# Product-key router of a 2-layer mixer block: the remaining up tiles beside the router in joined form, leading weights on VectorE, every second low part on GpSimd

## The chip, the core and the metric

One core of a Trainium2 chip runs the whole program. The metric is device time in microseconds (us), the median of three runs. Engines are called by the profile's names: PE is TensorE (PEld its weight loads), DVE is VectorE, ACT is ScalarE, POOL is GpSimd, SP is the queue that issues the weight transfers from HBM.

## The reference

Two stacks of two layers are run one after the other on 256 tokens of width 1024. The first stack has a product-key expert layer (PEER) after each mixer, and the change touches those two alone. Cut to what matters:

```python
def peer_mixer(h, w_query, sub_keys, w_up, w_down):
    q = (xc @ w_query).reshape(c, 8, 2, 128)
    sc = einsum('chpd,hpnd->chpn', q, keys32)
    sv, si = top_k(sc, 16)
    cand = sv[:, :, 0, :, None] + sv[:, :, 1, None, :]
    best, pos = top_k(cand, 16)
    eidx = ...                       # one of 128 x 128 experts, 8 x 16 of them a token
    g = softmax(best)
    a = einsum('cd,chkd->chk', xc, w_up[eidx])
    act = gelu(a) * g
    return einsum('chk,chkd->cd', act, w_down[eidx])
```

## The kernel before

**Dense experts.** The kernel does not gather. It computes `a` for all 16384 experts and multiplies by a weight that is zero for those not chosen. An "up tile" t (0 to 127) is 128 experts: its 128x1024 weights are loaded as one unit of 512 KB by SP into `raw`, a ring of 4. The program computes in fp32 accuracy with split numbers: ACT copies `raw` into `wh` (the high part, `high(n)`, line 1525), DVE writes `wl = raw - wh` (the low part, `low(n)`, line 2000). `wh` and `wl` are rings of two. The tokens are split in the same way and lie side by side in `x_both`. PE makes wh x high tokens, wh x low tokens and wl x high tokens.

**Two forms of an up tile** (`up(t)`). The joined form multiplies each of the 8 slices of `wh` with high and low tokens in one matmul of 512 columns (line 1148), then the 8 slices of `wl` with the high tokens, 256 columns each (line 1152). The bank then holds two halves that must be added: ACT copies both to `halves` (`copy_halves`, line 1650), POOL adds them (line 837, or line 849 into `late_sum`), and ACT applies gelu. The separate form runs 16 + 8 matmuls of 256 columns (line 1160) that all add up in one half, and ACT applies gelu right out of the bank.

**The stage of the change.** Tiles 72 to 127 (`FIRST` is 72) run beside the router. Of these, `LATE_JOINED` holds the even ones from 72 to 124, so 27 of the 56 tiles are joined and 29 separate, turn by turn. The router turns the chosen keys and weights of 4 tokens (a "quad", 64 in all) into a 128x128 table of weights for each token: it is a product of two one-hot matrices, one of them multiplied by the weight in three bf16 parts. For a quad, `build(q)` on DVE makes the one-hots (line 2318) and puts on the second and third part (two instructions, line 2324); `weigh_first(q)` on ACT puts on the leading part (four instructions, line 1719); PE makes 12 matmuls (`router(q)`, line 1189); ACT moves weights of later tiles to `acts` (`hold`, line 1727); DVE multiplies what is there already (`weigh`, line 2334, reading a PSUM bank) and tile by tile the rest (`late_weigh`, line 2343). The one-hots are a ring of 4 quads (`RING`), the weighted ones of 3 (`FIRSTS`), the router's banks of 4 (`OUTS`). The router of 2 or 3 quads stands in PE's order after every second (odd) tile: `quads_after(k)`.

**Order.** Every engine runs its own instructions in the order of the code. In the loop over `k` (tile 72 + k) ACT runs: copy or gelu of the tile, `weigh_first` of the next quads, `high` of tile + 2, late gelu of a joined tile, `hold`. DVE runs: `build` of the quads of slot k + 1, `low` of tile + 1, then at every second k `weigh` of 2 or 3 quads, then `late_weigh` of the tile before. POOL only adds the halves. SP loads a unit again when `lo_ready` has counted the unit four before it. After the stage come the down tiles (line 1176), which need all weights to be in place.

Of the kernel before, what the change touches and what calls it, by code (L numbers as in the profile page):

```python
# [13 lines left out]
F32 = mybir.dt.float32  # L14
# [8 lines left out]
P = 128  # L23
# [68 lines left out]
RING, FIRSTS, OUTS = 4, 3, 4  # L92
FIRST, SLOTS = 72, 54
APART = (range(22, 30), range(52, 60))
LATE_JOINED = range(FIRST, N_KEYS - 2, 2)
SPANS = ((0, 22), (22, 30), (30, 52), (52, 60), (60, FIRST))
EXP_TILES, SUM_TILES, CHOICE_TILES = (26, 54), (31, 61), (35, 63)
WIDE, NARROW = 4, 4
# [159 lines left out]
def build(nc, d, out):  # L258
    ctx = ExitStack()
    with ctx:  # L260
# [5 lines left out]
        def sem(name):  # L266
            if name not in sems:
                sems[name] = ctx.enter_context(nc.semaphore(name))
            return sems[name]
# [55 lines left out]
        at = place_of["aux"]  # L325
        lanes = place("lanes", [P, N_KEYS], BF16, at)
        at += 2 * N_KEYS
        weight_high = place("weight_high", [P, SEQ], F32, at)
        at += 4 * SEQ
        key_pairs = place("key_pairs", [P, SEQ, 2, 2], BF16, at)  # L330
        at += 2 * 4 * SEQ
        rest_pairs = place("rest_pairs", [P, 2, SEQ, 2], BF16, at)
        at += 2 * 4 * SEQ
        onehot = place("onehot", [P, RING, QUAD, 2, N_KEYS], BF16, at)
        at += 2 * RING * QUAD * 2 * N_KEYS
        first = place("first", [P, FIRSTS, 3, QUAD, N_KEYS], BF16, at)
# [205 lines left out]
        top_ready, top_exp = sem("top_ready"), sem("top_exp")  # L542
        top_split = sem("choices_split")
        onehots, first_weighted = sem("onehots_ready"), sem("first_keys_weighted")
        rests_weighted = sem("first_keys_weighted_by_rests")
        products, weighted = sem("router_products"), sem("experts_weighted")
        held, late_weighted = sem("router_weights_held"), sem("late_experts_weighted")
        gelu_done = sem("gelu_done")
# [229 lines left out]
        def _(pool):  # L778
# [47 lines left out]
            for layer, done in enumerate(("wo", "conv")):  # L826
                row_scales(f"peer{layer}")

                pool.dma_start(view(P_KEYS, HP, N_KEYS), d["keysT"][layer])\
                    .then_inc(extra_loaded["keys"], 16)  # L830
                pool.wait_ge(x_low, XG[f"rescaled{layer}"] + 4)
                pool.dma_start(lanes[:], d["c_lanes"].partition_broadcast(P)).then_inc(extra_loaded["lanes"], 16)

                def sum_halves(t, i=0):

                    pool.wait_ge(up_copied, unit_wait(joined(layer, t) + 1, i))
                    pool.tensor_tensor(acts[:, bass.ds(i * 4 + t, 1), :].rearrange("p a b -> p (a b)"), halves[:, 0], halves[:, 1], ALU.add)\  # L837
                        .then_inc(up_summed, 1)

                for c0, c1 in SPANS:  # L840
                    if together(c0):
                        with pool.Fori(0, (c1 - c0) // 4) as i:
                            for t in range(c0, c0 + 4):
                                sum_halves(t, i)
                        for t in range(c1 - (c1 - c0) % 4, c1):
                            sum_halves(t)
                for t in LATE_JOINED:
                    pool.wait_ge(up_copied, joined(layer, t) + 1)
                    pool.tensor_tensor(late_sum[:], halves[:, 0], halves[:, 1], ALU.add).then_inc(up_summed, 1)
                dump(done)  # L850
                if layer == 1:

                    pool.wait_ge(weighted, QUADS * (layer + 1))
                    pool.dma_start(gain_bc, d["norm_final"].partition_broadcast(P)).then_inc(extra_loaded["gain"], 16)
                    pool.dma_start(inv_freq, d["c_inv_freq"].partition_broadcast(P)).then_inc(extra_loaded["masks"], 16)
                    pool.dma_start(causal, d["c_causal"]).then_inc(extra_loaded["masks"], 16)
                    pool.dma_start(cmp_mask, d["c_cmp_mask"]).then_inc(extra_loaded["masks"], 16)
                    pool.wait_ge(units_used, first_unit["down1"] + HALF)
                    for t in range(TT):
                        pool.dma_start(view(0, TT, D)[:, t, :], d["mem"][t * P:(t + 1) * P, :])\  # L860
                            .then_inc(extra_loaded["mem"], 16)
                    row_scales("mem")
                row_scales(("conv", "between")[layer])
                dump(("peer0", "peer1")[layer])
# [30 lines left out]
        def _(pe):  # L895
# [213 lines left out]
            def peer(layer):  # L1109
# [27 lines left out]
                def up(t, i=0):  # L1137

                    n, b = u0 + t, t % 2
                    w = [x[:, n % SPLIT, :].rearrange("p (k e) -> p k e", k=KT) for x in (wh, wl)]  # L1140
                    if t >= 2 and together(t - 2):
                        pe.wait_ge(up_copied, unit_wait(joined(layer, t - 1), i))
                    elif t >= 2:
                        pe.wait_ge(gelu_done, unit_wait(N_KEYS * layer + t - 1, i))
                    if together(t):
                        pe.wait_ge(hi_ready, unit_wait(n + 1, i))
                        for k in range(KT):
                            pe.matmul(banks[b].rearrange("p (a b) -> p a b", a=2), lhsT=w[0][:, k, :], rhs=x_both[:, :, k, :],  # L1148
                                      start=k == 0, stop=False, skip_group_check=True)
                        pe.wait_ge(lo_ready, unit_wait(n + 1, i))  # L1150
                        for k in range(KT):
                            last = pe.matmul(banks[b][:, 0:SEQ], lhsT=w[1][:, k, :], rhs=xh[:, k, :], start=False, stop=k == KT - 1,  # L1152
                                             skip_group_check=True)
                        last.then_inc(units_used, 1)
                        return
                    for part in range(2):
                        pe.wait_ge((hi_ready, lo_ready)[part], unit_wait(n + 1, i))
                        for k in range(KT):
                            for xp in range(2 - part):
                                last = pe.matmul(banks[b][:, 0:SEQ], lhsT=w[part][:, k, :], rhs=x_in[xp][:, k, :],  # L1160
                                                 start=(k == 0 and part == 0 and xp == 0), stop=(k == KT - 1 and part == 1))
                    last.then_inc(units_used, 1)
# [18 lines left out]
                def router(q):  # L1181

                    pe.wait_ge(first_weighted, q0 + q + 1)
                    pe.wait_ge(rests_weighted, q0 + q + 1)
                    if q >= OUTS:
                        pe.wait_ge(weighted, q0 + q - OUTS + 1)
                    for c in range(QUAD):
# [317 lines left out]
        def _(act):  # L1505
# [113 lines left out]
            def peer(layer):  # L1619
# [89 lines left out]
                        ins = act.activation(acts[:, t, n:SEQ], src[:, n:SEQ], ACT.Gelu)  # L1709
                    ins.then_inc(gelu_done, 1)  # L1710

                def weigh_first(q):

                    act.wait_ge(onehots, q0 + q + 1)
                    if q >= FIRSTS:
                        act.wait_ge(products, q0 + q - FIRSTS + 1)
                    for c in range(QUAD):
                        c0 = q * QUAD + c
                        ins = act.activation(first[:, q % FIRSTS, 0, c, :], onehot[:, q % RING, c, 0, :], ACT.Copy,  # L1719
                                             scale=weight_high[:, c0:c0 + 1])  # L1720
                    ins.then_inc(first_weighted, 1)

                def hold(q):

                    n = tiles_before(q)
# [11 lines left out]
                    src = acts[:, bass.ds(i * 4 + t, 1), :].rearrange("p a b -> p (a b)")  # L1737
                    act.activation(gated_parts(layer, t)[0], src, ACT.Copy).then_inc(g_high, 1)

                for q in quads_in(0):  # L1740
                    weigh_first(q)
                for k in range(N_KEYS - FIRST):
                    if FIRST + k in LATE_JOINED:
                        copy_halves(FIRST + k)
# [2 lines left out]
                    if FIRST + k == N_KEYS - 2:  # L1747
                        act.wait_ge(weighted, q0 + QUADS)
                        gated_high(0)
                    for q in quads_in(k + 1):  # L1750
                        weigh_first(q)
                    high(u0 + FIRST + k + SPLIT)
                    if FIRST + k in LATE_JOINED:
                        late_gelu(FIRST + k)
# [224 lines left out]
        def _(dve):  # L1979
# [139 lines left out]
            def peer(layer):  # L2119
# [118 lines left out]
                def weights_of(t):  # L2238

                    cols = slice(t * P, (t + 1) * P)  # L2240
                    dve.tensor_copy(weight_high[:, cols], rounded[:])
                    step(tt(rest_of, choice[:, 2], rounded[:], ALU.subtract))
                    step(dve.tensor_copy(rest_pairs[:, 0, cols], rest_of.unsqueeze(2).to_broadcast([P, P, 2])))
                    step(tt(rest_of, rest_of, rest_pairs[:, 0, cols, 0], ALU.subtract))
                    step(dve.tensor_copy(rest_pairs[:, 1, cols], rest_of.unsqueeze(2).to_broadcast([P, P, 2])))

                wait_read(dve, J.of(f"scores{layer}", 7))
                dve.wait_ge(extra_loaded["lanes"], 16 * (layer + 1))
# [60 lines left out]
                def build(q):  # L2309
# [9 lines left out]
                    dve.wait_ge(onehots, q0 + q + 1)  # L2319
                    if q >= FIRSTS:  # L2320
                        dve.wait_ge(products, q0 + q - FIRSTS + 1)
                    for p in range(2):
                        rest_w = rest_pairs[:, p, c0:c0 + QUAD].unsqueeze(2).to_broadcast([P, QUAD, w, 2])
                        last = tt(first[:, q % FIRSTS, 1 + p].rearrange("p c (n b) -> p c n b", b=2),  # L2324
                                  onehot[:, s, :, 0].rearrange("p c (n b) -> p c n b", b=2), rest_w, ALU.mult)
                    last.then_inc(rests_weighted, 1)

                def weigh(q):

# [25 lines left out]
                for k in range(N_KEYS - FIRST):  # L2355
                    for q in quads_in(k + 1):
                        build(q)
                    low(u0 + FIRST + k + 1)
                    if k:
                        for q in quads_after(k - 1):  # L2360
                            weigh(q)
# [586 lines left out]
```

## Time and profile before

| | |
|---|---|
| median of 3 runs | 2298.92 us (2298.03 to 2300.6) |
| profiled execution | 2300.05 us |
| its span | 2298.2 us |
| busy PE / PEld / DVE / ACT / POOL | 2281.4 / 1996.9 / 1677.7 / 1404.6 / 181.4 us |
| chain that ended last | PE 92%, DVE 5%, issue 1%, ACT 1% |

"Busy" is the time in which an engine had at least one instruction under way. Matmuls overlap, so a busy PE is not a PE at its peak: the distance between starts says what one costs. The same holds on a smaller scale for DVE, whose next instruction starts some 80 ns before the end of the last. The chain follows the last instruction back, at each step to what released it. The stage beside the router occupies 387.4 to 591.9 us in the first PEER layer and 1295.0 to 1499.5 us in the second.

### The profile page before, as it was taken

What the parts mean: (1) busy time and instruction counts of PE and PEld (TensorE: products, weight loads), DVE (VectorE), ACT (ScalarE), POOL (GpSimd) and SP (SyncE); (2) the same over time, 40 slices, a digit from 0 to 9 for tenths busy, and PEclk for the clock granted to TensorE, in tenths of its full rate; (3) what the DMA queues carried; (4) which work ended last, traced back from release to release, by engine and by line L of the source; (5) the groups of instructions that cost most, each with busy time, mean ns of one, the idle gap of its engine ahead of it and who ended that gap; (6) DMA issues with size and microseconds to landing.
All of it is one profiled execution on the core that took longest, in us unless ns stands there. A gap on an engine that the chain in (4) does not pass through costs nothing.

```text
span 2298.2 us, 42511 instructions
## 1 busy us (share of the span) xinstructions
PE 2281.4 (99%) x14253; PEld 1996.9 (87%) x14253; DVE 1677.7 (73%) x3045; ACT 1404.6 (61%) x2618; POOL 181.4 (8%) x257
## 2 busy tenths in 40 slices
PE   9999999999999999999999999999999999999998
PEld 8799999999888888999899999988888888788777
DVE  6767997999655555775999799966555668767565
ACT  5657666888544455446666788844555555665554
POOL 1002121111000000000211211100000010000000
PEclk9999999999999999999999999999999999999999
DMA  7455666444566666566566544466666654346454
GB/s 244 146 185 163 187 183 181 142 144 141 184 193 193 195 192 192 177 183 192 168 182 190 166 141 146 147 207 192 191 211 181 194 187 136 86 139 197 131 165 146
DMA packets 137470, 397.50 MB, mean 173 GB/s; under 512 B 12480, under 2 KB 13808, under 8 KB 136560
## 3 DMA queue, kind: packets, MB, share of 16 engines
q1 hardware_dynamic: 134448, 384.71, 54.9%
q0 software_dynamic: 2448, 10.56, 1.4%
q8 instruction: 86, 1.41, 0.2%
q14 instruction: 56, 0.46, 0.1%
q10 hardware_dynamic: 432, 0.36, 0.0%
HBM read 394.54 MB, written 1.05 MB: 172 GB/s over the span
## 4 chain that ended last, share of the span: by engine, by line
PE 92%; DVE 5%; issue 1%; ACT 1%; DVEq 0%; POOLq 0%; POOL 0%; ACTq 0%
PE bank L1176 29%; PE bank L1148 13%; PE bank L1004 13%; PE bank L1160 11%; PE bank L1010 7%; PE bank L1152 7%; PE bank L1189 4%; DVE wl L2000 2%; PE bank L1036 1%; PE bank L1252 1%; PE bank L1104 1%; PE bank L1128 1%; PE bank L1015 0%; DVE aux L2038 0%; PE bank L1080 0%
## 5 line engine op out<-in xcount | busy, mean ns | idle before, releaser
L2000 DVE TENSOR_TENSOR wl<-raw,wh 128x1024 fp32r<-128x1024 f32 x726 | 886.8, 1223 | 501.2 <-ACT wh L1525 488.3
L1525 ACT ACTIVATE wh<-raw 128x1024 fp32r<-128x1024 f32 x725 | 764.4, 1055 | 602.2 <-PE bank L1176 327.7
L1148 PE MATMUL bank<-x_both,wh 128*128 128x512 f32 x1328 | 337.4, 396 | 0.0
L1148 PEld LDWEIGHTS bank<-x_both,wh 128*128 128x128 f32 x1328 | 238.2, 189 | 42.7
L1176 PE MATMUL bank<-wh,gl 128*128 128x512 f32 x992 | 265.6, 389 | 0.0
L1176 PE MATMUL bank<-wh,gh 128*128 128x512 f32 x992 | 265.3, 389 | 0.0
L1176 PE MATMUL bank<-wl,gh 128*128 128x512 f32 x992 | 265.2, 389 | 0.0
L1176 PEld LDWEIGHTS bank<-wh,gl 128*128 128x128 f32 x992 | 185.9, 188 | 39.5 <-DVE gl L2349 1.0
L1176 PEld LDWEIGHTS bank<-wl,gh 128*128 128x128 f32 x992 | 186.2, 188 | 38.8
L1176 PEld LDWEIGHTS bank<-wh,gh 128*128 128x128 f32 x992 | 186.0, 188 | 38.4
L1004 PE MATMUL bank<-wh,x_both 128*128 128x512 f32 (+1 forms) x768 | 195.9, 397 | 0.2 <-DVE x_both L2046 0.2
L1152 PEld LDWEIGHTS bank<-x_both,wl 128*128 128x128 f32 x1328 | 180.8, 190 | 14.6 <-DVE wl L2000 1.7
L1650 ACT ACTIVATE halves<-bank 128x512 f32<-128x512 f32 x166 | 99.3, 598 | 150.4 <-PE bank L1152 150.1
L1160 PE MATMUL bank<-x_both,wh 128*128 128x256 f32 x1440 | 188.3, 284 | 0.1
L1152 PE MATMUL bank<-x_both,wl 128*128 128x256 f32 x1328 | 185.5, 282 | 0.1
L1160 PEld LDWEIGHTS bank<-x_both,wh 128*128 128x128 f32 x1440 | 179.0, 192 | 1.0 <-ACT arena L1643 0.9
L1004 PEld LDWEIGHTS bank<-wh,x_both 128*128 128x128 f32 x768 | 140.0, 189 | 33.4 <-issue 6.3
L1719 ACT ACTIVATE first<-onehot,weight_high 128x128 bf16<-128x128 bf16 x512 | 160.7, 394 | 1.7 <-PE bank L1189 1.5
L2324 DVE TENSOR_TENSOR first<-onehot,rest_pairs 128x512 bf16<-128x512 bf16 x256 | 100.4, 433 | 20.3 <-PE bank L1189 16.3
L837 POOL TENSOR_TENSOR arena<-halves 128x256 f32 (+1 forms) x112 | 85.5, 763 | 358.2 <-ACT halves L1650 358.2
L2349 DVE TENSOR_TENSOR gl<-arena,gh 128x256 fp32r<-128x256 f32 x252 | 105.3, 418 | 0.0
L1004 PE MATMUL bank<-wl,x_both 128*128 128x512 f32 (+1 forms) x384 | 103.0, 390 | 0.0
(334 smaller groups left out, 2876.8 us busy)
## 6 DMA issues: line engine op xcount, KB each, us to landing
raw<-in_w_upT SPq DMA_DIRECT2D x256, 512.0 KB, 3.6
raw<-in_w_down SPq DMA_DIRECT2D x256, 512.0 KB, 3.7
raw<-in_l_w_in SPq DMA_DIRECT2D x84, 512.0 KB, 3.7
raw<-in_peer_w_query SPq DMA_DIRECT2D x32, 512.0 KB, 3.8
raw<-in_l_w_out SPq DMA_DIRECT2D x28, 512.0 KB, 3.7
raw<-in_conv_w_in SPq DMA_DIRECT2D x24, 512.0 KB, 3.8
raw<-in_attn_w_qkv SPq DMA_DIRECT2D x23, 512.0 KB, 4.6
arena<-in_na_bias POOLq DMA_DIRECT2D x4, 1024.0 KB, 6.2
```

The costliest lines, as they stand in the source:

```text
L1004: last = pe.matmul(bank(js[b])[:, 0:cols], lhsT=x[:, kt, b * P:(b + 1) * P], rhs=w[part][:, kk, :], **flags)
L1010: last = pe.matmul(bank(js[b])[:, m * SEQ:(m + 1) * SEQ], lhsT=w[part][:, kk, c0:c0 + P], rhs=x[:, kt, :], **f)
L1148: pe.matmul(banks[b].rearrange("p (a b) -> p a b", a=2), lhsT=w[0][:, k, :], rhs=x_both[:, :, k, :], start=k == 0, stop=False, skip_group_ ...
L1152: last = pe.matmul(banks[b][:, 0:SEQ], lhsT=w[1][:, k, :], rhs=xh[:, k, :], start=False, stop=k == KT - 1, skip_group_check=True)
L1160: last = pe.matmul(banks[b][:, 0:SEQ], lhsT=w[part][:, k, :], rhs=x_in[xp][:, k, :], start=(k == 0 and part == 0 and xp == 0), stop=(k == ...
L1176: last = pe.matmul(banks[4 + 2 * m + h][:, :], lhsT=g[gp][:, m * P:(m + 1) * P], rhs=w[:, h * 512:(h + 1) * 512], start=start and part == ...
L1525: act.activation(unit_parts(n)[0][:, 0:kts * cols], raw[:, n % RAW, 0:kts * cols], ACT.Copy)\
L1650: act.activation(halves[:].rearrange("p a b -> p (a b)"), banks[t % 2][:, :], ACT.Copy).then_inc(up_copied, 1)
L1719: ins = act.activation(first[:, q % FIRSTS, 0, c, :], onehot[:, q % RING, c, 0, :], ACT.Copy, scale=weight_high[:, c0:c0 + 1])
L2000: tt(lo[:, 0:kts * cols], raw[:, n % RAW, 0:kts * cols], hi[:, 0:kts * cols].bitcast(F32), ALU.subtract)\
L2324: last = tt(first[:, q % FIRSTS, 1 + p].rearrange("p c (n b) -> p c n b", b=2), onehot[:, s, :, 0].rearrange("p c (n b) -> p c n b", b=2), ...
L2349: tt(lo, src, hi.bitcast(F32), ALU.subtract).then_inc(g_low, 1)
```

## The change

The joined form is used for all tiles from 72 to 125 (54 in place of 27). The leading part of the router's weights is put on by DVE together with the two others, as a third instruction of the same shape, and no longer by ACT in four. The low part of the odd tiles 75 to 125 (`LATE_POOL`, 26 tiles in each layer) is computed by POOL, after it has added the halves of the tile two before. DVE waits for that before the low part of the next tile and counts it in `lo_ready`, so that SP sees the units in order.

```diff
-LATE_JOINED = range(FIRST, N_KEYS - 2, 2)
+LATE_JOINED = range(FIRST, N_KEYS - 2)
+LATE_POOL = range(FIRST + 3, N_KEYS - 2, 2)
...
                 for t in LATE_JOINED:
                     pool.wait_ge(up_copied, joined(layer, t) + 1)
                     pool.tensor_tensor(late_sum[:], halves[:, 0], halves[:, 1], ALU.add).then_inc(up_summed, 1)
+                    if t + SPLIT in LATE_POOL:
+                        n = first_unit[f"up{layer}"] + t + SPLIT
+                        pool.wait_ge(hi_ready, n + 1)
+                        hi, lo = unit_parts(n)
+                        pool.tensor_tensor(lo, raw[:, n % RAW, :], hi.bitcast(F32), ALU.subtract).then_inc(late_low, 1)
...
-                        pe.wait_ge(lo_ready, unit_wait(n + 1, i))
+                        if t in LATE_POOL:
+                            pe.wait_ge(late_low, len(LATE_POOL) * layer + LATE_POOL.index(t) + 1)
+                        else:
+                            pe.wait_ge(lo_ready, unit_wait(n + 1, i))
...
                     pe.wait_ge(first_weighted, q0 + q + 1)
-                    pe.wait_ge(rests_weighted, q0 + q + 1)
...
-                def weigh_first(q):
-
-                    act.wait_ge(onehots, q0 + q + 1)
-                    if q >= FIRSTS:
-                        act.wait_ge(products, q0 + q - FIRSTS + 1)
-                    for c in range(QUAD):
-                        c0 = q * QUAD + c
-                        ins = act.activation(first[:, q % FIRSTS, 0, c, :], onehot[:, q % RING, c, 0, :], ACT.Copy,
-                                             scale=weight_high[:, c0:c0 + 1])
-                    ins.then_inc(first_weighted, 1)
...
-                for q in quads_in(0):
-                    weigh_first(q)
...
-                    for q in quads_in(k + 1):
-                        weigh_first(q)
...
-                    dve.tensor_copy(weight_high[:, cols], rounded[:])
+                    dve.tensor_copy(weight_pairs[:, 0, cols], rounded[:].unsqueeze(2).to_broadcast([P, P, 2]))
...
-                    for p in range(2):
-                        rest_w = rest_pairs[:, p, c0:c0 + QUAD].unsqueeze(2).to_broadcast([P, QUAD, w, 2])
-                        last = tt(first[:, q % FIRSTS, 1 + p].rearrange("p c (n b) -> p c n b", b=2),
-                                  onehot[:, s, :, 0].rearrange("p c (n b) -> p c n b", b=2), rest_w, ALU.mult)
-                    last.then_inc(rests_weighted, 1)
+                    for p in range(3):
+                        by_weight = weight_pairs[:, p, c0:c0 + QUAD].unsqueeze(2).to_broadcast([P, QUAD, w, 2])
+                        last = tt(first[:, q % FIRSTS, p].rearrange("p c (n b) -> p c n b", b=2),
+                                  onehot[:, s, :, 0].rearrange("p c (n b) -> p c n b", b=2), by_weight, ALU.mult)
+                    last.then_inc(first_weighted, 1)
...
                 for k in range(N_KEYS - FIRST):
                     for q in quads_in(k + 1):
                         build(q)
-                    low(u0 + FIRST + k + 1)
+                    if FIRST + k in LATE_POOL:
+                        dve.wait_ge(late_low, len(LATE_POOL) * layer + LATE_POOL.index(FIRST + k) + 1)
+                        dve.nop().then_inc(lo_ready, 1)
+                    if FIRST + k + 1 not in LATE_POOL:
+                        low(u0 + FIRST + k + 1)
```

The tables `weight_high` (fp32) and `rest_pairs` become one table `weight_pairs` with three parts in bf16, each value twice.

## Rows read from the trace of the kernel before

**Rows 1.** The page: busy tenths and granted clock in 40 slices of the span

```profile
PE   9999999999999999999999999999999999999998
...
DVE  6767997999655555775999799966555668767565
ACT  5657666888544455446666788844555555665554
POOL 1002121111000000000211211100000010000000
PEclk9999999999999999999999999999999999999999
```

**Rows 2.** Busy time of each engine in both stages (start:end, length, busy)

```profile
387.40:591.90 204.50, 204.34 (x1898) 193.52 (x1897) 192.03 (x360) 175.02 (x514) 26.46 (x28) 1.00 0.49 148
1295.00:1499.50 204.50, 204.34 (x1898) 193.50 (x1897) 191.98 (x360) 175.03 (x514) 28.55 (x32) 1.00 0.48 148
```

**Rows 3.** PE in order of time, one joined and one separate tile (start, length)

```profile
395.11 2.08 PE L1148 MATMUL bank<-x_both,wh 128*128 128x512 f32 x8
397.03 1.12 PE L1152 MATMUL bank<-x_both,wl 128*128 128x256 f32 x8
397.98 2.08 PE L1160 MATMUL bank<-x_both,wh 128*128 128x256 f32 x16
399.90 1.12 PE L1160 MATMUL bank<-x_both,wl 128*128 128x256 f32 x8
400.86 1.51 PE L1189 MATMUL bank<-first,onehot 128*128 128x128 bf16 x24
402.19 2.08 PE L1148 MATMUL bank<-x_both,wh 128*128 128x512 f32 x8
```

**Rows 4.** PE in order of time, joined tiles that follow joined tiles

```profile
290.90 2.00 PE L1148 MATMUL bank<-x_both,wh 128*128 128x512 f32 x8
292.74 1.11 PE L1152 MATMUL bank<-x_both,wl 128*128 128x256 f32 x8
293.69 2.00 PE L1148 MATMUL bank<-x_both,wh 128*128 128x512 f32 x8
```

**Rows 5.** DVE's instructions in the first stage by line (busy, mean ns, idle before)

```profile
L2000 DVE TENSOR_TENSOR wl<-raw,wh 128x1024 fp32r<-128x1024 f32 x57 | 70.0, 1229 | 2.4 <-ACT wh L1525 2.2
L2324 DVE TENSOR_TENSOR first<-onehot,rest_pairs 128x512 bf16<-128x512 bf16 x124 | 48.2, 430 | 10.0 <-PE bank L1189 8.1
L2334 DVE TENSOR_TENSOR arena<-bank,arena 128x292 f32<-128x292 f32 (+31 forms) x64 | 32.9, 562 | 0.0
```

**Rows 6.** DVE and POOL in order of time, undisturbed

```profile
411.52 0.76 DVE L2324 TENSOR_TENSOR first<-onehot,rest_pairs 128x512 bf16<-128x512 bf16 x2
412.19 1.22 DVE L2000 TENSOR_TENSOR wl<-raw,wh 128x1024 fp32r<-128x1024 f32 x1
413.33 1.25 DVE L2334 TENSOR_TENSOR arena<-bank,arena 128x308 f32<-128x308 f32 x3
413.69 0.74 POOL L849 TENSOR_TENSOR late_sum<-halves 128x256 f32<-128x256 f32 x1 [6.38 <-ACT halves L1650]
```

**Rows 7.** The same, where POOL comes during an instruction of DVE

```profile
405.49 1.22 DVE L2000 TENSOR_TENSOR wl<-raw,wh 128x1024 fp32r<-128x1024 f32 x1
405.94 1.37 POOL L849 TENSOR_TENSOR late_sum<-halves 128x256 f32<-128x256 f32 x1 [6.22 <-ACT halves L1650]
```

**Rows 8.** The same, where DVE starts while POOL is at work

```profile
442.73 0.81 POOL L849 TENSOR_TENSOR late_sum<-halves 128x256 f32<-128x256 f32 x1 [6.34 <-ACT halves L1650]
442.85 1.23 DVE L2318 TENSOR_TENSOR onehot<-lanes,key_pairs 128x1024 bf16<-128x1024 bf16 x1
444.12 0.76 DVE L2324 TENSOR_TENSOR first<-onehot,rest_pairs 128x512 bf16<-128x512 bf16 x2
444.80 0.68 DVE L2318 TENSOR_TENSOR onehot<-lanes,key_pairs 128x1024 bf16<-128x1024 bf16 x1
```

**Rows 9.** POOL's and ACT's instructions by line and shape, whole span and first stage

```profile
L837 POOL TENSOR_TENSOR arena<-halves 128x256 f32<-128x256 f32 x8 | 6.0, 745 | 16.0 <-ACT halves L1650 16.0
...
L800 POOL TENSOR_TENSOR small<-small 128x2 f32<-128x2 f32 x1 | 0.2, 196 | 0.1
...
L1719 ACT ACTIVATE first<-onehot,weight_high 128x128 bf16<-128x128 bf16 x256 | 80.4, 394 | 0.9 <-PE bank L1189 0.7
L1525 ACT ACTIVATE wh<-raw 128x1024 fp32r<-128x1024 f32 x56 | 58.8, 1051 | 0.0
L1650 ACT ACTIVATE halves<-bank 128x512 f32<-128x512 f32 x28 | 16.7, 597 | 26.1 <-PE bank L1152 26.0
```

More of the change, by code:

```diff
@@ L327, in build @@
         at += 2 * N_KEYS
-        weight_high = place("weight_high", [P, SEQ], F32, at)
-        at += 4 * SEQ
         key_pairs = place("key_pairs", [P, SEQ, 2, 2], BF16, at)
         at += 2 * 4 * SEQ
-        rest_pairs = place("rest_pairs", [P, 2, SEQ, 2], BF16, at)
-        at += 2 * 4 * SEQ
+        weight_pairs = place("weight_pairs", [P, 3, SEQ, 2], BF16, at)
+        at += 2 * 6 * SEQ
         onehot = place("onehot", [P, RING, QUAD, 2, N_KEYS], BF16, at)
@@ L544, in build @@
         onehots, first_weighted = sem("onehots_ready"), sem("first_keys_weighted")
-        rests_weighted = sem("first_keys_weighted_by_rests")
+        late_low = sem("late_unit_low_by_gpsimd")
         products, weighted = sem("router_products"), sem("experts_weighted")
@@ L2240, in weights_of @@
                     cols = slice(t * P, (t + 1) * P)
-                    dve.tensor_copy(weight_high[:, cols], rounded[:])
+                    dve.tensor_copy(weight_pairs[:, 0, cols], rounded[:].unsqueeze(2).to_broadcast([P, P, 2]))
                     step(tt(rest_of, choice[:, 2], rounded[:], ALU.subtract))
-                    step(dve.tensor_copy(rest_pairs[:, 0, cols], rest_of.unsqueeze(2).to_broadcast([P, P, 2])))
-                    step(tt(rest_of, rest_of, rest_pairs[:, 0, cols, 0], ALU.subtract))
-                    step(dve.tensor_copy(rest_pairs[:, 1, cols], rest_of.unsqueeze(2).to_broadcast([P, P, 2])))
+                    step(dve.tensor_copy(weight_pairs[:, 1, cols], rest_of.unsqueeze(2).to_broadcast([P, P, 2])))
+                    step(tt(rest_of, rest_of, weight_pairs[:, 1, cols, 0], ALU.subtract))
+                    step(dve.tensor_copy(weight_pairs[:, 2, cols], rest_of.unsqueeze(2).to_broadcast([P, P, 2])))
                 wait_read(dve, J.of(f"scores{layer}", 7))
```

## The prediction, made before the changed kernel ran

> **What bounds the kernel now.** I read the slices of the page first [rows 1]: PE is in its top tenth nearly everywhere, at a granted clock in the top tenth too, and DVE comes up to it in two stretches, which are the two stages beside the router. The busy times of these stages come next [rows 2]. Each lasts 204.5 us. PE is busy for 204.3 of them, DVE for 192.0, ACT for 175.0, POOL for 26 to 29, and the clock is 1.00. So PE sets the end, and DVE has only 12.5 us to spare in each. The two stages agree within 0.1 us, so I work out one and take it twice.
>
> PE busy is not enough, so I take the distances of starts [rows 3]. A joined tile runs from 395.11 to 397.98, 2.87 us; a separate one from 397.98 to 400.86, 2.88 us; the router takes 1.33 us for two quads (400.86 to 402.19), so 0.665 a quad. 56 x 2.875 + 64 x 0.665 = 203.6 us: the stage holds under 1 us of stall. PE really is the bound, and what the change gives must come from PE or is lost.
>
> **What PE gains.** A joined tile that follows fp32 work, not the router, takes 2.79 us (290.90 to 293.69) [rows 4]. The odd tiles that change form stand behind a joined tile, so they should go from 2.88 to 2.79: 0.09 x 27 tiles = 2.4 us a layer, 4.9 us in all. That is the whole gain on the bound. The number of columns through PE is the same in both forms; only some weight loads go.
>
> **What ACT gains and pays.** It loses 4 x 64 instructions of 394 ns by the page, of which 80.4 us are busy [rows 9], and takes 27 more copies of 597 ns (16 us). It was not the bound before and is less so after: 175 - 80 + 16 = 111 us. The smaller edits go with this: the third table entry is one DVE copy a half layer ahead of the stage, one of PE's two waits goes, and the idle instruction of DVE that counts `lo_ready` computes nothing. I put them at nothing; if uncovered they would be well under 1 us.
>
> **What DVE alone gains.** A low part costs it 1.14 us (412.19 to 413.33) and one instruction that puts on a weight 0.335 us (two from 411.52 to 412.19) [rows 6]. 26 low parts go (29.6 us), 64 weight instructions come (21.4 us). Counted alone DVE falls from 192.0 to 183.8 us. If that were all, the change would be a small gain.
>
> **What POOL takes.** Rows of an undisturbed sum of 256 columns give 0.74 us [rows 6], 745 ns as a mean of eight [rows 9]; two columns take 196 ns [rows 9]. That is 2.14 ns a column, so the low part with its 1024 columns should take 0.20 + 1022 x 0.00214 = 2.38 us. Nothing of that size ran on POOL before. As bounds: with the whole 0.74 us paid by column it is 2.96 us, with no column cost beyond that of DVE's 1.14 us it is 1.2 us. I take 2.38, since two shapes of the same operation carry it. POOL's own load is 27 more sums of 0.74 and 26 low parts of 2.38, 82 us on top of 26: it has the time.
>
> **What POOL takes from DVE.** This is the term that decides. A sum of POOL that comes in the middle of a low part of DVE takes 1.37 us in place of 0.74: it started at 405.94, DVE's low part ended at 406.71, and POOL ended 0.60 later [rows 7]. In the other direction DVE's one-hot instruction, 0.68 us otherwise (the last of the group), takes 1.23 us when it starts 0.12 us into a sum: 0.55 us more [rows 8]. So the two exclude each other, and a sum of 256 columns holds DVE up by about 0.55 us, which is 256 times those 2.14 ns. Beside `weigh`, which reads one operand from PSUM, POOL's sum keeps its 0.74 us [rows 6]. All other work of DVE in this stage (one-hots, weights, low parts, late weights) has both operands in SBUF.
>
> The same is a rule of the Trainium skill, page "SBUF — State Buffer", section "SBUF: two separate sides": the shared pair is an exclusive lock, held for the whole instruction by a DVE operation with two SBUF inputs or by a GpSimd operation, and the loser fully blocks. By that rule the trace agrees (0.55 us and 0.60 us above), and it speaks against this change: what leaves DVE's queue for POOL still stops DVE. "GPSIMD Engine Reference", section 3.1, has 4497 ns for 2048 columns; half of that, an estimate of 2.25 us for the low part, would make the sum below 2 x 26 x 0.13 = 7 us smaller.
>
> **The sum.** What must not overlap in a stage: DVE's 183.8 us, less some 2.2 us of such collisions that its busy time already holds (means of 1229 and 430 ns against 1219 and 422 [rows 5], and two one-hots of 1.23), is 181.6. To it come 54 sums of 0.55 (29.4 us) and 26 low parts of 2.38 - 0.20 = 2.18 (56.7 us): 267.7 us. Only `weigh` can hide any: 32.9 us busy [rows 5], some 27.4 after its overlaps of 80 ns. That gives a floor of 240.3 us, if POOL worked beside every `weigh`, and 267.7 if beside none. Both are above the 202 us that PE needs.
>
> Where between? I follow a pair of tiles, o (odd) and e (even). DVE's order is: build, wait for POOL's low part of o, low part of e, late weigh, build, weigh, late weigh. Say DVE's low part of e ends at 0. PE finishes e 0.95 later and the copy ends near 1.9; DVE has then done its late weigh and its build (0.2 + 2.1), so POOL's sum of e falls on `weigh`, hidden. PE finishes the next odd tile at 0.95 + 2.8 = 3.75; copy and `high` (0.60 + 1.05 [rows 9], and gaps) release POOL's next low part at some 5.7, when DVE has left `weigh` and is in the next build or before the next low part. That one is not hidden, nor the sum of the odd tile. So 27 sums (15 us) hide: 253 us. DVE now idles 12.5 us a stage, 8.1 of it for the router's products [rows 5]; with DVE behind, I leave 4 of these. Forecast: 257 us a stage, 52.5 us more than 204.5. Pairs of tiles would go from 7.1 to about 9.5 us. Twice that is 105 us on the profiled 2300.05 us: 2405. The profiled run lies 1.1 us above the median of 2298.92, so 2404 us.
>
> **Who waits for the new waits.** DVE's wait for `late_low` has a low part, late weigh and the builds of the next quads behind it, and PE waits for those. It costs little of its own in the forecast, since POOL's low part is released by a tile that PE finished two tiles before. SP sees `lo_ready` later, but loads four units ahead with landings of under 4 us against pairs of 9.5: nothing.
>
> **The rivals.** (a) *Exclusion does not bind, chance 0.08.* POOL's low parts fall on `weigh` and on DVE's idle 12.5 us, or the long operation lets DVE through. Then PE stays the bound, and the time is 2300 - 4.9 = 2295 us. For it: DVE's queue alone gets shorter. Against: `weigh` and idle time together are 40 us, POOL holds 86. It needs each low part to hold DVE for less than about 0.7 us, where the sums' 0.55 us for a quarter of the size says 2.2. (b) *Best packing, chance 0.12.* POOL's low parts fall beside `weigh`, and the stage is 240 to 248 us: 2370 to 2387. (c) *Worst packing, chance 0.12.* Nothing hides and the in-order waits stay as they are, 12.5 us: 280 us a stage, 2451 us; more if POOL's low part is late behind builds of DVE and PE then stands in the middle of a tile. It decides where POOL's low part ends after PE's high part of that tile. (d) *POOL costs 2.96 us a low part, chance 0.03*: 26 x 0.58 = 15 us more a stage, 2434.
>
> **How the numbers follow.** The forecast's own case (exclusion, partly hidden, 2387 to 2425) has 0.65. Range: from 2366 (floor, less a few us for the smaller price of the low part) to 2446 (nearly all exposed). It leaves out (a) and half of (c) and little else. Under 0.2% (4.6 us) a measurement of this kernel can hardly tell from no change. Faster by more needs (a) in full: 0.05. Within 0.2%: 0.03, the rest of (a) and a gain eaten by waits. Slower: 0.92, all the other cases.
>
> **What the profile after would show.** Right: the stages last 245 to 270 us, POOL has instructions of 128x1024 with some 2.4 us undisturbed and over 3 us behind a DVE instruction, means of DVE's one-hot, weight and low instructions rise by tenths of a us, PEld of the wl part waits for DVE and POOL, PE has gaps of over 1 us a pair, and the granted clock stays 1.00. Wrong: stages of 202 us with odd tiles of 2.79 us, or DVE instructions of unchanged length beside a running low part of POOL. A fall of PE's clock in its new gaps would add to the time; no row shows one, as PE is never idle for long here.

## The result

The changed kernel takes 2444.49 us (median of 4 runs, 2443.68 to 2446.85) against 2299.2 us of the kernel before: a ratio of 1.0635, 95% interval 1.0623 to 1.0647. It is 145 us slower. The prediction was 2404 us with a range of 2366 to 2446. Sign and range hold, but only just: the time lies 1.5 us inside the end of the range, and one of the four runs lies outside it. 105 us were forecast and 145 came.

The page of the kernel after, its slices. Beside [rows 1], PE has fallen below its top tenth in the two stretches of the router, POOL has risen there, and the granted clock is no longer in its top tenth all along:

```profile
PE   9999998878899999999999888889999999999998
...
DVE  6758988999855555676898899985655667767665
...
POOL 1002113444300000000211344430000000000000
PEclk9999999989899999999999998989999999999999
```

Busy time in the two stages, which answers to [rows 2]. The columns after start:end are length, then busy time and count of PE, PEld, DVE, ACT and POOL, then granted clock, DMA share and GB/s:

```profile
387.60:663.60 276.00, 226.24 (x1688) 197.24 (x1689) 256.35 (x396) 121.56 (x285) 115.40 (x81) 0.91 0.36 109
1366.90:1643.30 276.40, 226.72 (x1689) 197.87 (x1690) 256.46 (x396) 121.73 (x285) 117.64 (x85) 0.91 0.36 110
```

The whole difference is here: 204.5 us have become 276.2, 71.7 more, twice 143.4 of the 145 us. DVE's busy time rose from 192.0 to 256.4 us, though it was given less to compute. PE has 50 us in which it does nothing. The clock is 0.91 where it was 1.00.

PE in order of time, two tiles of the first stage, beside [rows 3] and [rows 4]:

```profile
405.37 2.08 PE L1152 MATMUL bank<-x_both,wh 128*128 128x512 f32 x8
407.30 1.11 PE L1159 MATMUL bank<-x_both,wl 128*128 128x256 f32 x8
408.25 2.00 PE L1152 MATMUL bank<-x_both,wh 128*128 128x512 f32 x8
410.09 1.11 PE L1159 MATMUL bank<-x_both,wl 128*128 128x256 f32 x8
411.04 1.12 PE L1195 MATMUL bank<-first,onehot 128*128 128x128 bf16 x17
```

The odd tile, in its new form, takes 2.79 us (408.25 to 411.04) in place of 2.88. The gain of the change on the old bound is there, and it is as small as forecast.

DVE and POOL in the first stage by line (busy, mean ns, idle before and what ended it), beside [rows 5] and [rows 9]:

```profile
L2315 DVE TENSOR_TENSOR first<-onehot,weight_pairs 128x512 bf16<-128x512 bf16 x186 | 118.6, 692 | 16.1 <-PE bank L1195 14.2
...
L853 POOL TENSOR_TENSOR wl<-raw,wh 128x1024 fp32r<-128x1024 f32 x26 | 69.1, 2658 | 3.1 <-ACT wh L1531 2.9
...
L2309 DVE TENSOR_TENSOR onehot<-lanes,key_pairs 128x1024 bf16<-128x1024 bf16 x62 | 48.9, 788 | 0.0
L848 POOL TENSOR_TENSOR late_sum<-halves 128x256 f32<-128x256 f32 x54 | 45.8, 847 | 149.7 <-ACT halves L1656 149.6
...
L1991 DVE TENSOR_TENSOR wl<-raw,wh 128x1024 fp32r<-128x1024 f32 x31 | 43.1, 1392 | 3.5 <-ACT wh L1531 3.5
L2325 DVE TENSOR_TENSOR arena<-bank,arena 128x292 f32<-128x292 f32 (+31 forms) x64 | 32.9, 562 | 0.0
L2334 DVE TENSOR_TENSOR arena<-late,arena 128x8 f32<-128x8 f32 (+52 forms) x53 | 26.9, 508 | 0.0
```

Every DVE operation with both operands in SBUF has grown in the mean: weights from 430 to 692 ns, late weights (L2334 here) from 291 to 508, one-hots from 693 to 788, low parts from 1229 to 1392. The weighing (L2325), which reads PSUM, has kept its 562 ns. And this is the cause in two pairs of lines, DVE and POOL in order of time (start, length):

```profile
504.23 2.43 POOL L853 TENSOR_TENSOR wl<-raw,wh 128x1024 fp32r<-128x1024 f32 x1
504.32 2.89 DVE L2309 TENSOR_TENSOR onehot<-lanes,key_pairs 128x1024 bf16<-128x1024 bf16 x1
...
510.66 2.58 POOL L853 TENSOR_TENSOR wl<-raw,wh 128x1024 fp32r<-128x1024 f32 x1 [0.20 <-ACT wh L1531]
511.04 3.15 DVE L2315 TENSOR_TENSOR first<-onehot,weight_pairs 128x512 bf16<-128x512 bf16 x3
```

A one-hot instruction of 0.68 us takes 2.89 when it starts 0.09 us into POOL's low part: 2.21 us more. POOL's low part takes 2.43 us here. The prediction had 2.38 us for it and 2.18 us for what it holds.

What PE and DVE waited for in this stage (us in total, times, longest):

```profile
PE bank L1159 <- DVE wl L1991: 45.8, 18, 5.0
DVE first L2315 <- PE bank L1195: 14.2, 7, 3.2
```

PE's gaps are nearly all waits for DVE's own low parts, which stand in DVE's queue behind the builds. No wait for POOL's low part is listed for either engine.

### The profile page after: what moved, and what is told of

The parts are those of the page before. It is cut to its first block, busy times and chain, and to the rows that moved or that the text cites. A ratio compares the mean times of both kernels' runs of the same rounds, so it can differ in the third digit from the quotient of the medians.

```text
span 2441.9 us, 41347 instructions
## 1 busy us (share of the span) xinstructions
PE 2323.9 (95%) x13821; PEld 2003.3 (82%) x13821; DVE 1807.1 (74%) x3121; ACT 1297.8 (53%) x2160; POOL 357.7 (15%) x363
## 4 chain that ended last, share of the span: by engine, by line
PE 79%; DVE 16%; issue 4%; ACT 1%; DVEq 0%; POOL 0%; POOLq 0%; ACTq 0%
PE bank L1183 28%; PE bank L1008 12%; PE bank L1152 11%; PE bank L1014 7%; PE bank L1159 7%; DVE first L2315 5%; PE bank L1167 4%; DVE wl L1991 3%; DVE onehot L2309 2%; DVE arena L2325 1%; PE bank L1195 1%; PE bank L1040 1%; DVE arena L2334 1%; PE bank L1258 1%; PE bank L1108 1%
## 5 line engine op out<-in xcount | busy, mean ns | idle before, releaser
L1991 DVE TENSOR_TENSOR wl<-raw,wh 128x1024 fp32r<-128x1024 f32 x674 | 833.2, 1238 | 503.0 <-ACT wh L1531 490.9
L1152 PE MATMUL bank<-x_both,wh 128*128 128x512 f32 x1760 | 470.2, 411 | 0.0
L1152 PEld LDWEIGHTS bank<-x_both,wh 128*128 128x128 f32 x1760 | 335.3, 200 | 62.4
L1159 PEld LDWEIGHTS bank<-x_both,wl 128*128 128x128 f32 x1760 | 249.5, 200 | 121.8 <-DVE wl L1991 106.7
L1159 PE MATMUL bank<-x_both,wl 128*128 128x256 f32 x1760 | 262.4, 294 | 91.4 <-DVE wl L1991 91.4
L1656 ACT ACTIVATE halves<-bank 128x512 f32<-128x512 f32 x220 | 131.6, 598 | 375.3 <-PE bank L1159 375.3
L2315 DVE TENSOR_TENSOR first<-onehot,weight_pairs 128x512 bf16<-128x512 bf16 x384 | 241.9, 684 | 32.7 <-PE bank L1195 28.8
L1183 PE MATMUL bank<-wl,gh 128*128 128x512 f32 x992 | 265.2, 389 | 0.0
L853 POOL TENSOR_TENSOR wl<-raw,wh 128x1024 fp32r<-128x1024 f32 x52 | 137.7, 2649 | 6.1 <-ACT wh L1531 5.4
L848 POOL TENSOR_TENSOR late_sum<-halves 128x256 f32<-128x256 f32 x108 | 91.9, 851 | 300.0 <-ACT halves L1656 299.8
L1195 PE MATMUL bank<-first,onehot 128*128 128x128 bf16 x1536 | 97.3, 221 | 10.5 <-DVE arena L2325 10.4
```

The source lines that it names most:

```text
L853: pool.tensor_tensor(lo, raw[:, n % RAW, :], hi.bitcast(F32), ALU.subtract).then_inc(late_low, 1)
L1183: last = pe.matmul(banks[4 + 2 * m + h][:, :], lhsT=g[gp][:, m * P:(m + 1) * P], rhs=w[:, h * 512:(h + 1) * 512], start=start and part == ...
L1195: last = pe.matmul(banks[2 + q % OUTS][:, c * N_KEYS:(c + 1) * N_KEYS], lhsT=onehot[:, q % RING, c, 1, :], rhs=first[:, q % FIRSTS, p, c, ...
L1656: act.activation(halves[:].rearrange("p a b -> p (a b)"), banks[t % 2][:, :], ACT.Copy).then_inc(up_copied, 1)
L1991: tt(lo[:, 0:kts * cols], raw[:, n % RAW, 0:kts * cols], hi[:, 0:kts * cols].bitcast(F32), ALU.subtract)\
L2315: last = tt(first[:, q % FIRSTS, p].rearrange("p c (n b) -> p c n b", b=2), onehot[:, s, :, 0].rearrange("p c (n b) -> p c n b", b=2), by_ ...
```

## The experiments

Two things were to be settled. Is the cost exclusion (DVE stopped while POOL reads) or waiting (PE and DVE late because POOL's low part is late)? And where do the 40 us beyond the forecast come from? The first four runs each do a part of the change alone or leave one out; the later ones edit the changed kernel. "Stage" is the first of the two throughout, taken from the profiled run, and times are medians of 4 runs each. Ratios are against the kernel before, run beside them (2299.1 to 2299.6 us).

**Everything but GpSimd's low parts.**

```diff
-LATE_POOL = range(FIRST + 3, N_KEYS - 2, 2)
+LATE_POOL = range(0)
```

> The changed kernel, but every low part is computed by VectorE again; all tiles 72 to 125 stay joined and VectorE still puts on all three parts of the router's weights. Exclusion (a VectorE operation with two SBUF inputs and a GpSimd operation never overlap): VectorE has 192.0 - 2.2 + 21.4 = 211.2 us of work a stage and 54 sums of 0.55 us (29.4 us) stop it, half of them hidden beside the weighing from PSUM: 226 us and some 12 us of waits, 238 a stage, about 2366 us in all. Rival (what costs is waiting for GpSimd's long low part, not exclusion): with that wait gone only VectorE's own 213 us and a few us of waits are left, 218 a stage, about 2326 us.

Measured: 2367.0 us, ratio 1.0296 (1.0279 to 1.0313), a stage of 238.6 us, of which DVE is busy for 225.9. The sum gave 238 and 2366, with 226 busy. Of the 145 us, 77 hang on the low parts' place and 68 are there without it. So the slowdown has more than one source, and the rival that knows only the wait is out by 41 us.

**The joined form alone.**

```diff
 (the kernel before)
-LATE_JOINED = range(FIRST, N_KEYS - 2, 2)
+LATE_JOINED = range(FIRST, N_KEYS - 2)
```

> The kernel before with the joined form for all tiles 72 to 125 and nothing else: ScalarE puts on the leading weights, VectorE computes all low parts. Exclusion: VectorE 189.8 us and 29.4 us of sums, of which some 11 us hide: 208 us and 8 us of waits, 216 a stage, about 2323 us. Rival (sums cost VectorE nothing, TensorE stays the bound): 0.09 us a tile is gained, 202 us a stage, 2294 us.

Measured: 2321.68 us, ratio 1.01 (1.0083 to 1.0117), a stage of 216.9 us. 27 short sums more on POOL turn a gain of 2.4 us a stage on PE into a loss of 12. DVE's busy time rises from 192.0 to 208.1 us, with not one instruction more on it, and it idles 8.8 us:

```profile
386.36:603.30 216.94, 206.39 (x1690) 181.55 (x1690) 208.15 (x360) 191.40 (x541) 53.88 (x56) 1.00 0.44 139
```

The joined form also brings ACT 27 copies, and no run has the sums without the copies. But 27 x 0.55 = 14.9 us is nearly the whole of DVE's 16 us.

**GpSimd's low parts alone.** The kernel before, with the new waits on PE and DVE, and on POOL:

```diff
+LATE_POOL = range(FIRST + 3, N_KEYS - 2, 2)
...
+                    if t + SPLIT in LATE_POOL:
+                        n = first_unit[f"up{layer}"] + t + SPLIT
+                        pool.wait_ge(hi_ready, n + 1)
+                        hi, lo = unit_parts(n)
+                        pool.tensor_tensor(lo, raw[:, n % RAW, :], hi.bitcast(F32), ALU.subtract).then_inc(late_low, 1)
```

> The kernel before with the low parts of the odd tiles 75 to 125 on GpSimd and nothing else. Exclusion: VectorE 192.0 - 29.6 - 2.2 = 160.2 us, sums 14.9 us, low parts of GpSimd 56.7 us: 231.8, less 8 hidden, with 12 to 18 us of waits: 236 to 242 a stage, 2362 to 2375 us. Rival (no exclusion, VectorE is relieved by 30 us): TensorE stays the bound at 204.5 a stage, 2300 us.

Measured: 2359.46 us, ratio 1.0264 (1.0246 to 1.0281), a stage of 234.1 us. It is 3 us below the lower end: DVE idled 6.3 us, less than the 12 to 18 allowed, while its busy time is 4 us above the 223.8 of the sum. DVE has 26 instructions less than before and is busy for 227.8 us in place of 192.0. Taking 30 us of work off DVE cost it 36.

**VectorE's third weight instruction alone.** The changed kernel with the two other parts taken back:

```diff
-LATE_JOINED = range(FIRST, N_KEYS - 2)
-LATE_POOL = range(FIRST + 3, N_KEYS - 2, 2)
+LATE_JOINED = range(FIRST, N_KEYS - 2, 2)
+LATE_POOL = range(0)
```

> The kernel before with all three parts of the weights put on by VectorE and nothing else: 27 joined tiles, all low parts on VectorE. VectorE 189.8 + 21.4 = 211.2 us, sums 14.9 us with 8 hidden: 218 us and 6 to 12 us of waits, 224 to 230 a stage, 2340 to 2351 us. Rival (waits of 12.5 us take up the added work): 205 to 213 a stage, 2300 to 2317 us.

Measured: 2338.27 us, ratio 1.0171 (1.0154 to 1.0188), 2 us below the lower end, with a stage of 224.1 us. DVE is busy for 212.9 us, 5 less than the sum had, and idles 11.2. Its 12.5 idle us of before did not take up the work; they stayed almost as they were.

The parts alone cost 22.2, 60.0 and 38.8 us, 121 together. The whole costs 145: together they are dearer by 24 us. The stretches in which PE's clock is at its lower level (below) are 48 us a stage in the whole and at most 7 in a part.

**GpSimd writes and doesn't read.** The test of exclusion itself: same place, same waits, nearly the same duration. This kernel leaves out the low parts of these tiles (they are zero).

```diff
+        pool_step, pool_steps = sem("pool_step"), [0]
...
-                        pool.tensor_tensor(lo, raw[:, n % RAW, :], hi.bitcast(F32), ALU.subtract).then_inc(late_low, 1)
+                        for width in (UNIT, UNIT, 256):
+                            ins = pool.memset(lo[:, 0:width].bitcast(F32), 0.0)
+                            pool_steps[0] += 1
+                            ins.then_inc(pool_step, 1)
+                            pool.wait_ge(pool_step, pool_steps[0])
+                        pool.nop().then_inc(late_low, 1)
```

> The changed kernel, with GpSimd's low part replaced by writing alone: three fills of the low tile (1024, 1024 and 256 columns, one after the other, some 2.4 us together), which read nothing from SBUF. The low parts of these tiles are zero in it, so part of the computation is left out; every wait and every engine's order stays. Exclusion between operations that read (what the Trainium skill, page 'SBUF - State Buffer', section 'SBUF: two separate sides', gives as the condition for a VectorE operation with two SBUF inputs): only the 54 sums stop VectorE, 181.6 + 29.4 - 15 us and some 12 us of waits, 208 a stage, 2308 us or so, and VectorE's instructions keep their length beside the fills. Rival 1 (exclusion against any GpSimd operation): about the changed kernel's 2444 us. Rival 2 (PE and VectorE wait for the late low part, whatever it does): also about 2440 us, but with VectorE's instructions at their own length and VectorE idle in front of the wait.

Measured: 2310.9 us, ratio 1.0053 (1.0036 to 1.007), a stage of 210.2 us. DVE and POOL in order of time:

```profile
507.61 2.33 POOL L855 MEMSET wl<- 128x1024 f32 x3
...
508.54 1.21 DVE L1997 TENSOR_TENSOR wl<-raw,wh 128x1024 fp32r<-128x1024 f32 x1
509.68 0.30 DVE L2340 TENSOR_TENSOR arena<-late,arena 128x144 f32<-128x144 f32 x1
```

DVE's low part of two SBUF operands keeps its 1.21 us beside the fill. With 2.33 us of POOL per tile before `late_low` is told, but nothing read, 134 of the 145 us are gone. So the new waits and a low part that arrives 2.33 us later cost next to nothing by themselves. The 134 us hang on POOL's reading: on the exclusion, and on what it sets off in PE's waits and clock (below). The 54 sums still read here, and are part of the 12 us that stay. This also is what the Trainium skill, page "SBUF — State Buffer", section "SBUF: two separate sides", states as the condition for such a VectorE operation: only a GpSimd operation that reads SBUF excludes it.

**TensorE's gaps filled.** What is left is the 40 us beyond the forecast. In the kernel after, PE in order of time:

```profile
515.38 2.07 PE L1159 MATMUL bank<-x_both,wl 128*128 128x256 f32 x8 [3.13 <-DVE wl L1991]
517.26 3.62 PE L1152 MATMUL bank<-x_both,wh 128*128 128x512 f32 x8
```

PE waits 3.13 us for DVE's low part, and then 8 wide matmuls take 3.62 us where they take 2.00 elsewhere. The stretch lies at the lower of the two clock levels (1.2 GHz in place of 2.4), as its granted clock of 0.50 shows, the third number from the end:

```profile
517.20:520.25 3.05, 3.05 (x10) 2.37 (x9) 3.02 (x7) 1.95 (x4) 0.74 (x1) 0.50 0.29 109
```

The trace records 11 such stretches in this stage, 48 us together, and none in either stage before. The next run gives PE something to do in front of these waits:

```diff
+                        if t in range(FIRST + 4, N_KEYS - 2, 2):
+                            for k in range(KT):
+                                pe.matmul(banks[7][:, :].rearrange("p (a b) -> p a b", a=2), lhsT=w[0][:, k, :], rhs=x_both[:, :, k, :],
+                                          start=k == 0, stop=k == KT - 1, skip_group_check=True)
                         if t in LATE_POOL:
```

> The changed kernel with 8 more matmuls of 512 columns, into a bank that nobody reads, between the high and the low part of every even tile from 76: 1.84 us of TensorE work where it waits for VectorE. If the stretches at the lower clock (11 in the first stage, 48 us together) lengthen the stage, they go, and the time falls by up to 2 x 15 us, to 2415. If VectorE and GpSimd alone set the pace, the clock rises and the time stays at 2444 us or grows by under 15 us where TensorE was late already.

Measured: 2421.49 us, ratio 1.0533 (1.0515 to 1.055). 25 groups of useless matmuls in a layer, 46 us of work, make the kernel 23 us faster, of the 2 x 15 that the expectation allowed at most. Its stage:

```profile
387.65:652.85 265.20, 252.68 (x1888) 219.03 (x1889) 253.67 (x396) 121.89 (x285) 118.85 (x81) 1.00 0.37 114
```

The clock is 1.00 again, the stage 265.2 us, and DVE idles 11.5 us in place of 19.7; its wait for the router's products is 7.2 us in place of 14.2.

**The low part in four pieces.**

```diff
-                        pool.tensor_tensor(lo, raw[:, n % RAW, :], hi.bitcast(F32), ALU.subtract).then_inc(late_low, 1)
+                        for c0 in range(0, UNIT, 256):
+                            ins = pool.tensor_tensor(lo[:, c0:c0 + 256], raw[:, n % RAW, c0:c0 + 256], hi[:, c0:c0 + 256].bitcast(F32),
+                                                     ALU.subtract)
+                        ins.then_inc(late_low, 1)
```

> The changed kernel with GpSimd's low part in four instructions of 256 columns. Exclusion as a sum: 4 x 0.55 = 2.2 us held, as before, 2435 to 2450 us. Rival (the length of one hold makes VectorE's and TensorE's waits, 18 us idle on VectorE a stage): VectorE gets in between the pieces, idle time falls to 12 us or less, 2430 us or lower. The other way: each piece waits behind a VectorE instruction of up to 1.2 us, the low part lands some 3 us later and TensorE waits for it: above 2455 us.

Measured: 2435.97 us (2432.05 to 2439.96), ratio 1.0591 (1.0574 to 1.0609). DVE is busy for 256.5 us as with one long instruction and idles 18.5 us. What counts for DVE's busy time is the sum of what POOL holds, not how it is cut; the 8 us gained go with 37.5 us at the lower clock in place of 48, which was not tested apart.

**VectorE's low part ahead of its builds.**

```diff
-                    for q in quads_in(k + 1):
-                        build(q)
                     if FIRST + k in LATE_POOL:
                         dve.wait_ge(late_low, len(LATE_POOL) * layer + LATE_POOL.index(FIRST + k) + 1)
                         dve.nop().then_inc(lo_ready, 1)
                     if FIRST + k + 1 not in LATE_POOL:
                         low(u0 + FIRST + k + 1)
+                    for q in quads_in(k + 1):
+                        build(q)
```

> The changed kernel with VectorE's wait for GpSimd and its own low part ahead of the one-hots and weights of the next quads, in each turn of the loop. TensorE waited 45 us a stage for VectorE's low parts of even tiles. If VectorE's idle 18 us come from TensorE being late with the router's products, they shrink to 8 or so: 2424 us. If the order only moves the wait from the low parts to the router's tables, 2440 to 2450 us.

Measured: 2419.78 us, ratio 1.0526 (1.0508 to 1.0543), even a little better than expected. DVE idles 8.8 us in a stage of 266.2. But PE still stands, now before the router, for what DVE has not yet built, and the clock is as low as before:

```profile
388.30:654.50 266.20, 224.44 (x1688) 197.14 (x1689) 257.42 (x396) 123.38 (x285) 123.33 (x81) 0.92 0.36 113
```

So in this order the lower clock cost nothing that the times show: 44 us of it lie in this stage, which is within 1 us of that of the filled kernel, and the next run confirms it by filling the gaps here too. In the changed kernel it did cost. The waits fit the reading that it costs where DVE waits for PE: DVE waited 14.2 us for the router's products there, 7.2 in the filled kernel, and here no such wait is listed.

**Both at once.** The matmuls of the filled kernel and the order of the last run together:

> The changed kernel with both edits that took 23 to 25 us each: the added matmuls on TensorE and VectorE's low part ahead of its builds. If the first works by the clock and the second by VectorE's waits, as two causes, the times add up: 2444.5 - 23 - 25 = 2397 us, stages of 254 us. That is near the floor of what must not overlap (240 us a stage with the weighing hidden, 2372 us). If both remove the same stall, 2418 us. If the added work now makes TensorE late for the router, above 2420.

Measured: 2420.5 us, ratio 1.053 (1.0512 to 1.0547), a stage of 263.8 us with DVE busy for 255.8. The granted clock is 0.99, and the time is that of the last run within 1 us. The two edits don't add up, against the first theory; the second, that both remove the same stall, had 2418 us. That stall is DVE's wait for a late PE, which is not listed here either. What remains is mostly DVE's own queue with what POOL takes from it, and 8.0 us of idle time. Whether the added matmuls cost a little of their own, as the third theory has it, can't be told from a difference of 1 us.

**Half of the low parts.**

```diff
-LATE_POOL = range(FIRST + 3, N_KEYS - 2, 2)
+LATE_POOL = range(FIRST + 3, N_KEYS - 2, 4)
```

> The changed kernel with GpSimd's low parts for every fourth tile from 75 (13 in each layer) and VectorE's for the others. One low part on VectorE costs 1.14 us of its time, one on GpSimd holds it for 2.18 or more. Exclusion as a plain sum: half way between no low part on GpSimd (2367.0 us) and 26 (2444.5 us), 2406 us; without the share of the lower clock, which comes with the idle gaps, nearer 2400. If each costs only through a wait that TensorE then meets, the first 13 could be free: 2370 to 2380 us.

Measured: 2400.39 us (2397.39 to 2402.45), ratio 1.0437 (1.0419 to 1.0454). The first 13 a layer cost 33 us, the next 13 cost 44. Already the first 13 are paid, at 1.3 us a piece (33.4 / 26); the sum's 1.04 us (2.18 less 1.14) is most of it. The theory that they are free, 2370 to 2380 us, is out. The stretches at the lower clock go from 14 us a stage without any to 27 and 48, and this fits the steeper second half, though nothing was run here that holds the clock with 13.

## Why the prediction was right, and where it was short

- **PE is the bound before, and gains 0.09 us a tile.** Right: 2.79 us measured for the odd tiles. It was never collected, since PE stopped being the bound.
- **POOL's low part: 2.38 us, holding 2.18.** Right: 2.43 us in the row shown (2.36 in the shortest of the 26), and DVE held for 2.21. Extrapolating from 2 and 256 columns to 1024 was sound. The mean of 2.66 us fits POOL's own waiting behind DVE; this was not tested apart.
- **Exclusion is the term that decides.** Right, and shown: a fill of nearly the same length that reads nothing leaves 12 of the 145 us. The rival that exclusion does not bind falls with it, and so does the explanation by the new waits alone.
- **DVE and POOL as one queue: 267.7 us less 15 hidden, 253.** Right: DVE was busy for 253.7 us in the filled kernel, 256.4 in the changed one. The low parts were hardly hidden, as the pair of tiles followed had it: of POOL's 69 us in them, 1.1 lay beside the weighing in the trace of the changed kernel.
- **DVE's idle time: 4 of 12.5 us.** This step failed. I argued that with DVE behind, waits for the router's products would shrink. In the kernels where DVE puts on all three parts of the weights they did not: DVE idled 12.7 us with the low parts on DVE, 11.2 with the weights alone, 11.5 in the filled kernel. Where ACT kept the leading part, idle time did shrink, to 8.8 us (joined form alone) and 6.3 (GpSimd's low parts alone), and it was 8.8 again with DVE's low part ahead of its builds. So how much of an idle time is slack depends on the order of the work around it; why it stayed in just these kernels, no run shows. At 7.5 us a stage this is 15 of the missing 40 us.
- **PE's clock.** The forecast put no term for it in the sum, and had "the granted clock stays 1.00" among the signs of being right; it said only that a fall in PE's new gaps would add to the time. The clock was 0.91. This is the other part: 11 us in the first stage and 10 in the second between the changed and the filled kernel, 23 us in the times. It acts through DVE's wait for PE, as far as the waits tell, and a better order of DVE's work removes it as well as a full PE does.

Against the forecast of 253 + 4 us a stage stand 253.7 us busy and 11.5 idle in the filled kernel, and 11 us more in the changed one: 276 us. The split between the last two depends on taking the filled kernel as the step between; they are not independent, as the new order of DVE's work took away 25 us in all with the clock as low as before.

That the range held is partly luck. The forecast's own case (2387 to 2425 us, chance 0.65) did not come true, nor did its sign of stages of 245 to 270 us. The end of the range came from the case "nothing hides and 12.5 us stay idle", 280 us a stage. The measured 276 us are another mix: some 11 to 14 us were hidden, idle time stayed, and the clock made up the difference. Some figures of the working are slightly off: 54 x 0.55 is 29.7 us, not 29.4; the collisions taken off come to 2.7 us by its own numbers, not 2.2; the weighing less 64 overlaps of 80 ns is 27.8 us, not 27.4; and 257 us over 28 pairs is 9.2 us, not 9.5. Together they move the forecast by less than 1 us.

## What to carry to other kernels

Before work goes from VectorE to GpSimd, look at what both read. If both read two operands from SBUF, count them as one engine: here each low part gave DVE 1.14 us and took 2.2. Look for rows in which a short GpSimd operation meets a VectorE one, and scale what it holds by its columns; that number told more than all busy shares. And when a sum makes another engine the bound, keep that engine's present idle time in it as one of the bounds until something shows which wait is gone, and add a line for what idle gaps do to TensorE's clock.

No version here beats the kernel before. Its stage of 204.5 us stands 1 us above PE's own 203.6, and the gain on PE that the joined form offers, 0.09 us a tile, costs DVE some 0.55 us a tile in sums.

## What the runs showed of the hardware beyond the prediction

A useless load can pay. 1.84 us of matmuls that nobody reads, in the even tiles from 76 before PE waits for DVE's low part, raised the granted clock from 0.91 to 1.00 and took 23 us off 2444; with DVE's work in the better order they took off nothing (2419.8 us without them, 2420.5 with). And a fill on GpSimd costs a VectorE operation with two SBUF operands nothing (a low part keeps its 1.21 us beside a fill of 2.33), where a subtraction of about the same length held a one-hot instruction for 2.21 us.
